# Grouping the modulation slabs of a fused two-block transformer kernel: pairs in the MLPs, fours in attention

## What is computed

```
m = (jax.nn.silu(cvec) @ w_mod + b_mod).reshape(-1, 1, N_MOD * D_MODEL)
sh1, sc1, g1, sh2, sc2, g2 = modulation(c, w_mod[l], b_mod[l])
csh1, csc1, cg1, csh2, csc2, cg2 = modulation(c_ctx, w_mod[l], b_mod[l])
```

```
s = einsum(qn, k_nope) + einsum(qr, k_rope)
prob = softmax(s * scale)
o = einsum('bhqk,bkhd->bqhd', prob, v)
h = jnp.square(jax.nn.relu(h @ w1)) @ w2
```

## Time and profile before

| | |
|---|---|
| median of 3 runs (lowest to highest) | 2794.37 us (2790.46 to 2797.18) |
| the profiled execution: time, span | 2792.76 us, 2790.9 us |
| TensorE (PE) busy, share of the span | 2694.9 us, 97% |
| VectorE (DVE), ScalarE (ACT), GpSimd (POOL) busy | 58%, 43%, 14% |
| share of PE in the chain that ended last | 89% |
| mean granted TensorE clock | 0.99 |
| slabs | 302 transfers of 1 MB on SP's queue, of 306 |

### The profile page before, as it was taken

How to read it: one execution, slowest core, us unless ns; L and a number is a source line. 1 busy time by engine, 2 the same in 40 slices (tenths; PEclk the granted TensorE clock), 3 DMA queues, 4 the chain that set the end, 5 groups by cost and what they waited for, 6 DMA issues and landing times.

```text
span 2790.9 us, 44915 instructions
## 1 busy us (share of the span) xinstructions
PE 2694.9 (97%) x17244; PEld 2280.6 (82%) x17244; DVE 1615.2 (58%) x2837; ACT 1191.1 (43%) x2232; POOL 400.7 (14%) x560
## 2 busy tenths in 40 slices
PE   6999999999998999999999999989999999998999
PEld 4756877778857998887789999978777788987999
DVE  4565634334765756985367777784433346457665
ACT  4343522224444445346355556653322234354443
POOL 0000000000000301000066666640000000024000
PEclk9999999999999999999999999999999999999999
DMA  7264244442363543323300000032444433210453
GB/s 292 77 238 154 106 179 164 170 180 95 117 247 138 176 180 136 136 91 110 113 5 1 2 1 2 1 122 100 156 181 169 163 134 134 76 61 32 165 180 136
DMA packets 49628, 343.57 MB, mean 123 GB/s; under 512 B 5296, under 2 KB 7344, under 8 KB 9776
## 3 DMA queue, kind: packets, MB, share of 16 engines
q1 hardware_dynamic: 44960, 324.03, 31.5%
q10 hardware_dynamic: 4496, 17.15, 1.6%
HBM read 333.82 MB, written 7.34 MB: 122 GB/s over the span
## 4 chain that ended last, share of the span: by engine, by line
PE 89%; DVE 6%; ACT 2%; DMA 1%; issue 1%; ACTq 0%; POOL 0%; DVEq 0%; SPq 0%
PE ps L763 21%; PE ps L765 20%; PE ps L764 20%; PE ps L2394 4%; PE ps L960 3%; PE ps L2381 3%; PE ps L2373 2%; PE ps L2402 1%; PE ps L1015 1%; PE ps L990 1%; DVE ring_rest L751 1%; PE ps L2429 1%; PE ps L2446 1%; PE ps L3233 1%; PE ps L2350 1%
## 5 line engine op out<-in xcount | busy, mean ns | idle before, releaser
L763 PE MATMUL ps<-hidden_high,w_high 128*128 128x256 f32 (+2 forms) x1208 | 399.1, 330 | 3.7 <-DVE ring_rest L751 2.2
L1411 ACT ACTIVATE w_high<-ring 128x2048 fp32r<-128x2048 f32 x124 | 236.9, 1911 | 380.7 <-DMA ring<-in_w_dram 257.1
L763 PE MATMUL ps<-h_high,w_high 128*128 128x256 f32 (+1 forms) x1056 | 355.2, 336 | 5.5 <-DVE h_low L737 3.5
L764 PE MATMUL ps<-h_low,w_high 128*128 128x256 f32 (+1 forms) x1056 | 351.8, 333 | 0.0
L764 PE MATMUL ps<-hidden_low,w_high 128*128 128x256 f32 (+1 forms) x1056 | 350.1, 331 | 0.0
L1894 DVE TENSOR_TENSOR mix_high<-ring,w_high 128x2048 fp32r<-128x2048 f32 x56 | 128.4, 2292 | 246.9 <-ACT w_high L1411 246.9
L765 PE MATMUL ps<-hidden_high,ring_rest 128*128 128x256 f32 (+2 forms) x872 | 263.0, 302 | 0.0
L763 PEld LDWEIGHTS ps<-hidden_high,w_high 128*128 128x128 f32 (+1 forms) x1208 | 229.1, 190 | 35.2 <-issue 10.8
L763 PEld LDWEIGHTS ps<-h_high,w_high 128*128 128x128 f32 x1056 | 202.5, 192 | 32.2 <-issue 11.5
L1894 DVE TENSOR_TENSOR ring_rest<-ring,w_high 128x2048 fp32r<-128x2048 f32 x68 | 157.2, 2312 | 123.6 <-ACT w_high L1411 123.6
L764 PEld LDWEIGHTS ps<-h_low,w_high 128*128 128x128 f32 x1056 | 202.6, 192 | 18.2
(11 more groups left out here) (504 smaller groups left out, 6222.1 us busy)
## 6 DMA issues: line engine op xcount, KB each, us to landing
ring<-in_w_dram SPq DMA_DIRECT2D x302, 1024.0 KB, 4.8
z_spill<-arena ACTq DMA_DIRECT2D x16, 256.0 KB, 2.0
arena<-z_spill SPq DMA_DIRECT2D x2, 2048.0 KB, 9.3
C<-in_first_dram ACTq DMA_DIRECT2D x1, 2432.0 KB, 11.1
X<-in_x_dram ACTq DMA_DIRECT2D x1, 2048.0 KB, 13.0
x_spill<-X ACTq DMA_DIRECT2D x1, 2048.0 KB, 10.1
X<-x_spill SPq DMA_DIRECT2D x1, 2048.0 KB, 7.8
C<-in_third_dram ACTq DMA_DIRECT2D x1, 2048.0 KB, 9.3
```

The costliest lines, as they stand in the source:

```text
L763: ins = nc.tensor.matmul(out_, w_high, high, start=first, stop=False)
L764: nc.tensor.matmul(out_, w_high, rest, start=False, stop=False)
L1411: nc.scalar.activation(W_HIGH[:, (j + 1) % 2, :], ring[:, s], ACT.Copy).then_inc(sems["w_high"], 1)
```

## The change

In attention, the modulation slabs of iterations i to i + 3 are issued together in iteration i, where i is a multiple of four. In the hosting MLPs, they are issued two at a time, behind own slabs 1, 3, 5 and 6, and the layout of the slabs in DRAM follows. The number of instructions of each kind, the ring, SP's rule and what ScalarE and VectorE do, and in what order, stay as they are.

```diff
-                if i < m:
-                    s = v.place(i)
-                    pe.wait_ge(landed[s], v.landed(i))
-                    if i % 4 == 0:
-                        pe.wait_ge(freed[6], v.free(6, i // 4))
-                    pe_slab_rows(v, s, 0, i)
+                if i < m and i % 4 == 0:
+                    for j in range(i, i + 4):
+                        s = v.place(j)
+                        pe.wait_ge(landed[s], v.landed(j))
+                        if j % 4 == 0:
+                            pe.wait_ge(freed[6], v.free(6, j // 4))
+                        pe_slab_rows(v, s, 0, j)
...
-        HOSTED = ((0,), (1,), (2,), (3,), (4,), (5,), (6, 7), ())
+        HOSTED = ((), (0, 1), (), (2, 3), (), (4, 5), (6, 7), ())
...
-            for j in range(6):
-                out += [own[j], more[j]]
-            out += [own[6], more[6], more[7], own[7]]
+            out += [own[0], own[1], more[0], more[1], own[2], own[3], more[2], more[3]]
+            out += [own[4], own[5], more[4], more[5], own[6], more[6], more[7], own[7]]
```

## The result

| | before | changed |
|---|---|---|
| device time, median of 4 runs | 2794.45 us (2790.46 to 2797.18) | 2844.49 us (2841.07 to 2849.95) |
| ratio, 95% interval | | 1.0177 [1.0165, 1.0188] |
| profiled execution: span | 2790.9 us | 2839.3 us |
| mean granted clock of TensorE | 0.990 | 0.985 |
| attention, from the first scores to the convolution's first transform, layer 0 / layer 1 | 87.67 / 57.05 us | 117.07 / 77.98 us |

The change makes the kernel 50 us slower, as forecast in sign; the forecast of 2830 us was 14 us short, inside its range of 2809 to 2848. The table says where to look: of 48.4 us of span, attention holds 29.4 + 20.9 = 50.3, the two hosting MLPs give 2.2 each back, and the rest is the start (0.5) and one more stretch of half clock near the end (2.0), in code that the change does not touch.

A forecast was written before the change was run, and what follows sets the result against it. TensorE, busy 97% of the span, was taken to bound the kernel; -6.2 (MLP merges) + 25 (late slab) + 6 (copy) + 2 (scaling) + 10 (clock) = +37 us on 2792.8 gave 2830 us, range 2809 to 2848.

The forecast's parts named there:

- The fourth slab of every block is late: Attention: TensorE waits 2.9 to 3.6 us, taken as 3.2, for slab i + 3 in each of ten groups; +25 us net of merges.
- the merges in attention: Attention: three of four slabs join a block and save 0.24 us each, -0.7 us a group.
- the copy of bank 6: Attention: the next block waits for ScalarE's copy of bank 6, 0.8 us in eight groups, +6 us.
- the clock: Attention: TensorE's clock halves behind eight of ten waits, 1.3 us a stretch, +10 us, bounds 0 and 16.
- Rival 1: Attention: the late-slab wait is there but the clock stays up; 2820 us, chance 20%.
- what the thinned iterations cost with 512 keys: Attention, iterations without a slab: TensorE's work and the chain of maximum, exponential and scaling both about 4.5 us a pair; nothing added.
- the pairs with 256 keys: Attention: four pairs of iterations with 256 keys and no slab include a 0.44 us wait for VectorE's scaling; +2 us.
- the feeding of the own slabs is not at risk: Hosting MLPs: own slab 3 still arrives and is split in time, 2.5 us to spare; 18 merges give -6.2 us.
- likeliest case: Whole kernel: the forecast's own case, late slabs, chains and clock within their bounds, 2820 to 2846 us; chance 65%.
- Rival 2: Attention: the fourth slab is no wait, merges alone act there and in the MLPs; 2779 us, chance 4%.
- rival 3: Attention: no difference, the wait is made up later because VectorE and ScalarE ran ahead; 2793 us, chance 3%.
- Rival 4: Attention: transfers issued behind slab i + 3 slow it, each wait 2.6 us longer, +26; 2856 us, chance 8%.

The follow-up runs named there:

- e2: Changed kernel, but TensorE reports a block's end at the first transpose behind it, so SP asks for the next fourth slab earlier; 1.0058 of the kernel before.
- e5: Changed kernel with ScalarE's copy of bank 6 two iterations earlier (4g + 1 instead of 4g + 3); 1.0138 of the kernel before.
- e10: Changed kernel with 13 unused 256-column products added in each attention block ahead of the wait for the fourth slab; 1.0235 of the kernel before.
- e12: Changed kernel with 6 unused 256-column products added in each attention block ahead of the wait for the fourth slab; 1.0147 of the kernel before.
- e1: Kernel before with only the change's MLP part, attention as before; 0.9984 of the kernel before.
- e4: Changed kernel with three slabs in iteration i and the fourth in iteration i + 1 in attention; 1.0040 of the kernel before.
- e6: Changed kernel with the slab asked for earlier and ScalarE's copy of bank 6 two iterations earlier; 1.0042 of the kernel before.
- e3: Changed kernel with modulation slabs in pairs, in every even iteration, in attention too; 1.0018 of the kernel before.
- e7: Attention as before, the MLPs' modulation slabs in pairs behind own slabs 0, 2, 4 and 6; 2786.54 us, 0.9963 of the kernel before.

## Why the prediction was right, and where it fell short

**Right: the sign, the place and the mechanism.** The fourth slab of every block is late by the chain as written: 0.77 to 0.79 us to the issue (0.79 forecast), 4.7 to 5.0 us to landing (4.7 to 5.4), gaps of 2.7 to 3.0 us (2.9 to 3.6, I took 3.2). Ten of them are 28.2 us, against 32. e2 shows that it is the cause: with the slab asked for earlier, 33 us come back, gaps and clock together. The estimate of 4.4 us for a landing, which the prediction worked out from the Trainium skill (DMA: Bandwidth & Descriptors, "Anatomy of one DMA"), is of transfers that GpSimd issues; these slabs are issued by SyncE, and the ten took 4.7 to 5.0 us.

**Right: the merges in attention.** -0.7 us a group; the undivided block of e2 gives 3.68 - 4.40 = -0.7.

**Right: the copy of bank 6.** +6 us forecast, 7.3 us of waits measured, in the eight groups named. e5, which moves the copy, is 10 us faster than the change.

**Right: the clock.** +10 us for eight stretches of 1.3; there are seven of 1.6, some 11 us by e10 and e12. Rival 1, that the clock stays up, falls: the ten gaps were 2.67 to 3.03 us long, and the granted clock fell to 0.50 behind seven of them. Which gaps would cost was not foreseen, and no run here explains it. The Trainium skill (TensorE: Matmul & The Clock Gate, "Why this matters for your kernels") warns of idle gaps between bursts of matmuls and names a length that lies among these ten. This trace does not bear that length out: the seven gaps with a fall behind them lasted 2.70 to 2.96 us, and the longest of the ten, 3.03 us, had none.

**Wrong: what the thinned iterations cost with 512 keys.** The step is "with 512 keys TensorE's own work in a pair is about 4.5 us and the chain of maximum, exponential and scaling about the same, so I add nothing", and +2 us for the pairs with 256 keys. Two lengths that are "about the same" do not hide each other: a few tenths more on one of them are a wait. The transposes' waits for the scaling went from 4 to 15 and from 2.2 to 7.3 us, +5.1 instead of +2: 3.9 us are in units with 512 keys, where I had nothing, and 1.1 in those with 256. The product with V waits 0.5 us more. And I had counted a wait as its idle time alone. In the change TensorE waits 40 times in attention instead of 10, and each wait costs the 0.07 to 0.21 us of lost overlap beside it, 4.6 us in sum.

With these terms the account closes. Adding up the steps from start to start of TensorE's instructions in attention, the change is 50.3 us over before: 40.8 of waits (28.2 ring, 7.1 copy, 5.1 scaling, 0.5 product with V), 11.2 clock, 4.6 lost overlap, -7.0 merges, and 0.7 left over. e2 is 20.4 over: 18.5 of waits, 5.1 clock (a stretch of 3.4 us and one of 6.8), 3.2 lost overlap, -7.0 merges, and 0.6 left over.

**Wrong: "the feeding of the own slabs is not at risk".** I checked own slab 3, whose place in the order moved, and not own slab 1, which lost what stood ahead of it. It cost 1.0 us in each MLP: -4.5 by e1 instead of -6.2.

**The sum, term by term.** Forecast: -6.2 + 25 + 6 + 2 + 10 = +37. Measured: -4.5 in the MLPs, 28.2 - 7 = 21 for the late slab, 7.1 copy, 5.1 + 0.5 for the scaling and the product with V, 11 clock, some 5 for lost overlap and the remainder: about +46. The profiled execution was 48.4 us longer; 2.0 of that are the half clock near its end and 0.5 its start. The late slab came out 4 us smaller than forecast. The miss is in what the thinned iterations cost (+5.6 against +2, and 1 more for the copy), in the lost overlap, which the sum did not have, and 1.7 us in the MLPs. The hit is a narrow one: with every wait and bound of the prediction at its highest the terms give 29 - 6.2 + 10 + 16 = +49, 2842 us, and the range went on to 2848; the median was 2844.5. The end of 2846 that the prediction gives for its likeliest case does not follow from its terms.

**The other rivals.** Rival 2 (the slab is no wait) and rival 3 (the wait is made up) fall by the ten gaps, in which VectorE stands still and ScalarE nearly so. Rival 4 (transfers share the queue) falls too: the slab that TensorE waits for took 5.0 us, those asked for behind it 6.6 and 8.2. The first is served first, or nearly.

Theory 1, that the late slab is nearly all, was the same mistake told again: it holds for some 39 of 50 us (28.2 and the clock), and the remainder, with e2 as the proof, is more than the merges give.

## What to carry to other kernels

Where a ring of n places is refilled by a count that the user's own first instruction gives, a group of n uses in a row finds its last one late, by the time to issue and landing less what the first n - 1 uses take (here 0.8 + 4.8 - 2.8 us); leave one use out of the group, or count the release where the place really comes free (28.2 us of waits became 4.3 in e4 and 5.9 in e2). And before work is gathered into one place, ask what it had been covering where it stood: here each merge gave 0.24 to 0.35 us, and the iterations that it emptied gave back more. Gather where the stream is dense on both sides (the MLPs), not where the small pieces fill the gaps of another chain, and look at the item that loses its predecessor, not only at the one that is moved. A wait costs its idle time and the overlap that the instruction behind it would have had, here 0.07 to 0.21 us each.

## What the runs showed of the hardware that I had not expected

- Adding work made the kernel faster. Six products in each gap kept the granted clock at 1.00 through attention, and the time came out 0.0030 lower (intervals that just touch; attention 5.4 us shorter in the profiled execution).
- Behind seven of ten waits of 2.67 to 3.03 us the granted clock fell to 0.50 for 3.4 us, behind three it did not, in one and the same loop. The length of a wait does not decide it: in e12 one of 2.37 us had no fall behind it, in e4 and e6 waits of 2.03 and 2.05 us had one, and in the kernel before, ahead of attention, so had this one of 1.67 us (the earlier trace rows are the products behind it):

```profile
104.35 0.39 PE L894 MATMUL ps<-arena,ones 32*128 32x128 f32 x4 [1.67 <-DVE arena L1611]
```

- A wait costs more than its idle time: 0.07 us behind scores ahead of a slab, 0.16 ahead of the transposes and the product with V, 0.21 between two slabs, since without a wait the next product starts before the last has ended.
- A product of 256 columns in full float32, with 96 rows, took 0.447 us in two passes (0.43 from start to start within a run of them), twice what I had sized it at.
- Stretches at half clock come and go between executions elsewhere too: there are 11 in the profiled execution before, 19 in that of the change, of which only seven are in attention, and 12 to 15 in those of e1, e2, e3 and e7, of which two in attention in all. Differences of 2 us between two profiled executions are therefore no evidence by themselves.
